# Two layers of a mixer and mixture-of-experts backbone on one core: an opening, a scan tail, a routing step and a gather put in another order

## The reference

```python
for l in range(DEPTH):
    sh1, sc1, g1, sh2, sc2, g2 = split(silu(c) @ w_ada[l] + b_ada[l], 6)     # modulation
    out = token_mixer(x * (1 + sc1) + sh1)         # attention, scan and gating branches
    x = layer_norm(alpha * x + g1 * out)
    ff = hier_moe(x * (1 + sc2) + sh2)             # 4 groups of 8 experts, two chosen
    x = layer_norm(alpha * x + g2 * ff)

def token_mixer(h):
    proj = h @ w_in                                # q, k, v, z, xbc, dt, u, gv, gates
    y_att, y_gm = attention(q, k, v), gelu(u) * spatial(layer_norm(gelu(gv)))
    y_ssm = rms_norm((scan(xbc, dt) + d * xs) * silu(z))
    return (g0 * (y_att @ wb[0]) + g1 * (y_ssm @ wb[1]) + g2 * (y_gm @ wb[2])) @ w_o
```

## Time and profile before

| | before |
|---|---|
| median of 3 runs (lowest, highest) | 1283.43 us (1276.03, 1285.51) |
| the profiled execution's own time | 1282.84 us |
| its span, first to last instruction | 1281.0 us |
| mean granted TensorE clock | 0.968 |
| PE busy | 1208.1 us (94%) |
| DVE busy | 971.0 us (76%) |
| ACT busy | 716.9 us (56%) |
| moved by DMA | 358.83 MB, mean 280 GB/s |

### The profile page before, as it was taken

How to read it: one execution, slowest core, us unless ns; L and a number is a source line. 1 busy time by engine, 2 the same in 40 slices (tenths; PEclk the granted TensorE clock), 3 DMA queues, 4 the chain that set the end, 5 groups by cost and what they waited for, 6 DMA issues and landing times.

```text
span 1281.0 us, 15755 instructions
## 1 busy us (share of the span) xinstructions
PE 1208.1 (94%) x5953; PEld 949.2 (74%) x5953; DVE 971.0 (76%) x1159; ACT 716.9 (56%) x684; POOL 74.5 (6%) x121
## 2 busy tenths in 40 slices
PE   4999999989989999999989999998998999999994
PEld 1667777877677888888767777776777888888883
DVE  1654657797689889888877475769857998888887
ACT  1543544553567777677753354445336776767773
POOL 0400000101000000000020000010000000000000
PEclk8899998999999999999989989989998999999998
DMA  9987763537899999999956767445348999999980
GB/s 355 291 287 274 296 229 139 184 137 273 333 356 363 375 369 353 347 370 346 343 166 227 293 242 282 163 139 175 136 169 306 369 397 354 357 338 371 347 321 34
DMA packets 99491, 358.83 MB, mean 280 GB/s; under 512 B 9188, under 2 KB 12736, under 8 KB 83024
## 3 DMA queue, kind: packets, MB, share of 16 engines
q1 hardware_dynamic: 87504, 295.12, 63.1%
q0 software_dynamic: 11904, 62.63, 13.9%
HBM read 352.92 MB, written 5.83 MB: 280 GB/s over the span
## 4 chain that ended last, share of the span: by engine, by line
PE 73%; DVE 11%; DMA 5%; ACT 4%; issue 2%; DVEq 2%; ACTq 1%; SPq 1%; POOL 0%; POOLq 0%
PE bank L950 69%; PE bank L953 4%; DVE wl L1826 4%; ACT wh L1521 2%; DMA adaw<-in_w_ada 2%; DMA first<-in_w_ada 1%; DMA raw<-in_w_in 1%; DVE tmp L1826 1%; DVE seg L2308 1%; DVEq L2333 1%; DMA decay<-decay_rows 1%; DVE xbc L2098 0%; DVE xbc L2095 0%; SPq L763 0%; DVE gv L1826 0%
## 5 line engine op out<-in xcount | busy, mean ns | idle before, releaser
L1826 DVE TENSOR_TENSOR wl<-raw,wh 128x2048 fp32r<-128x2048 f32 (+1 forms) x268 | 607.3, 2275 | 118.0 <-ACT wh L1521 64.6
L1731 ACT ACTIVATE wh<-raw 128x2048 fp32r<-128x2048 f32 x192 | 367.4, 1915 | 49.7 <-PE bank L950 34.9
L950 PE MATMUL bank<-wh,xgh 128*128 128x512 f32 x512 | 209.1, 408 | 0.6 <-ACT xgh L1766 0.6
L950 PE MATMUL bank<-wh,xgl 128*128 128x512 f32 x512 | 202.9, 396 | 0.0
L1521 ACT ACTIVATE wh<-raw 128x2048 fp32r<-128x2048 f32 (+1 forms) x76 | 142.2, 1872 | 103.8 <-PE bank L950 61.0
L950 PE MATMUL bank<-wh,hTh 128*128 128x512 f32 x448 | 184.5, 412 | 2.8 <-DVE wl L1826 2.0
L950 PE MATMUL bank<-wl,hTh 128*128 128x512 f32 x448 | 180.0, 402 | 0.0
L950 PE MATMUL bank<-wh,hTl 128*128 128x512 f32 x448 | 179.5, 401 | 0.0
L950 PE MATMUL bank<-wl,xgh 128*128 128x512 f32 x512 | 140.3, 395 | 0.0
L950 PEld LDWEIGHTS bank<-wl,xgh 128*128 128x128 f32 x512 | 96.0, 188 | 23.6 <-DVE wl L1826 0.4
L950 PEld LDWEIGHTS bank<-wh,xgh 128*128 128x128 f32 x512 | 96.8, 189 | 20.2 <-DVE xgl L1826 0.8
(11 more groups left out here) (301 smaller groups left out, 1465.6 us busy)
## 6 DMA issues: line engine op xcount, KB each, us to landing
raw<-in_moe_w SPq DMA_DIRECT2D x256, 512.0 KB, 5.6
raw<-in_moe_w SPq DMA_DIRECT2D x64, 1024.0 KB, 6.8
raw<-in_w_in SPq DMA_DIRECT2D x52, 1024.0 KB, 6.8
adaw<-in_w_ada POOLq DMA_DIRECT2D x32, 1024.0 KB, 6.7
raw<-in_w_branch SPq DMA_DIRECT2D x12, 1024.0 KB, 5.3
raw<-in_w_ada SPq DMA_DIRECT2D x8, 1024.0 KB, 9.9
raw<-in_w_o SPq DMA_DIRECT2D x8, 1024.0 KB, 4.9
first<-in_w_ada SPq DMA_DIRECT2D x4, 1024.0 KB, 16.7
```

What stands on the lines that cost most here:

```text
L950: return behind(nc.tensor.matmul(*args, **kw))
L1731: tally(A_(wh[c][:, :], slot[r], ACT.Copy), part_high[c])
L1826: return V.tensor_tensor(o, a, b, op)
```

## The change

Seven edits, in the order of the program:

1. SP fetches the last two `w_ada` chunks and the first q piece ahead of x, and x has semaphores of its own (`x_in`).
2. PE makes all eight chunks first; stream 0 of x is turned after them, stream 1 behind the first q products. ACT takes the modulation row ahead of the first q piece's high part, and makes the second piece's behind the first four rows of tokens; DVE does the modulation ahead of the first low part.
3. `scanned` no longer squares and sums on DVE; ACT does it (`squared`, an activation with an accumulator).
4. The low part of (2,1) moves on DVE from between the last two scan steps to behind `scanned(1)`.
5. PE makes half 1 of branch 2 for stream 0 ahead of turning z, and for stream 1 behind it.
6. The last two chunks of the next modulation move behind `rank` (layer 0); in layer 1 five mask products (`busy5`) stand there. ACT takes the row out behind the first two gathers of the loop.
7. The gate values' gather stands between the second and the third low product of expert 0's second half, not behind the products.

```diff
@@ sync, opening
-            sp.dma_start(x[:, 0, :], A["x_prompt"][0]).then_inc(once, 16)
-            sp.dma_start(x[:, 1, :], A["x_sample"][0]).then_inc(once, 16)
-            load(0, SLOTS)
             load_first(2)
             load_first(3)
+            load(0, SLOTS)
+            sp.dma_start(x[:, 0, :], A["x_prompt"][0]).then_inc(x_in[0], 16)
+            sp.dma_start(x[:, 1, :], A["x_sample"][0]).then_inc(x_in[1], 16)
@@ tensor
-            for key in ada(0, 0, 0, 6):
+            for key in ada(0, 0):
                 accumulate(0, "ada0", key)
-            pe.wait_ge(once, 48)
-            turn_x(0, "x1T")
-            for key in ada(0, 0, 6):
-                accumulate(0, "ada0", key)
+            pe.wait_ge(once, 16)
...
                 if l == 0:
+                    turn_x(l, "x1T", (0,))
                     turn_mod(l, 0, "adaT0")
                     keep_busy(l, "busy2", 6)
...
-                    if n == 1 and l:
+                    if n == 1:
                         turn_x(l, "x1T", (1,))
...
                 branch(l, 2, (0,))
+                branch(l, 2, (1,), (0,))
                 branch_rows(l, 1, z)
-                branch(l, 2, (1,))
+                branch(l, 2, (1,), (1,))
                 branch(l, 1)
...
                 turn_x(l, "x2T", (1,))
-                next_ada(6, 8)
                 pe.wait_ge(s0_act, 3 * l + 3)
...
                 fills(ins, "rank")
+                next_ada(6, 8)
+                if l == L - 1:
+                    keep_busy(l, "busy5", 5)
...
                             for c in range(4):
+                                if i == 0 and h == 1 and c == 2:
+                                    gather(tally, rnd, 0, SELECTED)
...
                             if rnd == 0 and l < L - 1:
                                 turn_mod(l, 0, "adaT_next")
-                            gather(tally, rnd, 0, SELECTED)
@@ scalar
-            convert_to(0, 0)
             take_row(0, 0, "ada0")
-            convert_to(0, 1)
+            convert_to(0, 0)
...
                         high(0, 2, 4)
+                        convert_to(l, 1)
...
+                def squared(s):
+                    act.wait_ge(z_scanned, 2 * l + s + 1)
+                    A_(tmp[:, NW:D], z[:, s, :], ACT.Square, accum_out=small[:, s:s + 1])
+                    act.drain().then_inc(z_squared, 1)
+                squared(0)
                 gate_take(1, 1)
                 branch_turned(2)
+                squared(1)
                 ahead(("branch", 2, 0))
                 square_root(1)
...
                 modulate("x2T", 1, lambda: root_of(0, 1))
-                if l < L - 1:
-                    take_row(l, 0, "ada_next")
...
                     gathered(0, 1)
+                    if rnd == 0 and l < L - 1:
+                        take_row(l, 0, "ada_next")
@@ vector
                 if l == 0:
+                    modulation(l, 0, "adaT0")
                     convert_to(0, 0)
-                    modulation(l, 0, "adaT0")
...
-                    tt(z[:, s, :], y, z[:, s, :], ALU.mult)
-                    drain()
-                    tt(tmp[:, NW:D], z[:, s, :], z[:, s, :], ALU.mult)
-                    drain()
-                    V.tensor_reduce(small[:, s:s + 1], tmp[:, NW:D], X, ALU.add)
-                    drain()
+                    tt(z[:, s, :], y, z[:, s, :], ALU.mult).then_inc(z_scanned, 1)
...
-                    if 1 <= n < 8:
+                    if 1 <= n < 7:
                         ahead(SCAN_FILL[n - 1])
...
                 scanned(1)
+                ahead(SCAN_FILL[6])
+                dve.wait_ge(z_squared, 2 * l + 2)
```

More of the change, by code:

```diff
@@ L240, in make_plan @@
         plan.append(("busy4", 4))
+        plan.append(("busy5", 4))
     plan.append(("rt", 5))
@@ L498, in hybrid_backbone @@
         once = sem("once")
+        x_in = [sem(f"x_in{s}") for s in range(2)]
         cond_in = sem("cond_in")
@@ L556, in hybrid_backbone @@
         y_sem = sem("y_sem")
+        z_scanned = sem("z_scanned")
+        z_squared = sem("z_squared")
         var_ready = sem("var_ready")
@@ L815, in _ @@
                 pool.wait_ge(first_in[i], 16)
+            for s in range(2):
+                pool.wait_ge(x_in[s], 16)
             for n in range(L):
@@ L1039, in turn_x @@
                 for s in streams:
-                    pe.wait_ge(x_norm[s], 2 * l + (which == "x2T") + 1)
+                    if l == 0 and which == "x1T":
+                        pe.wait_ge(x_in[s], 16)
+                    else:
+                        pe.wait_ge(x_norm[s], 2 * l + (which == "x2T") + 1)
                     xv = x[:, s, :].rearrange("t (p c) -> t c p", c=DC)
@@ L1094, in branch_rows, with branch @@
                     turn4(l, f"yT{b}{s}", [yv[:, c, :] for c in range(BC)])
-            def branch(l, b, halves_=(0, 1)):
+            def branch(l, b, halves_=(0, 1), streams=(0, 1)):
                 for n in halves_:
                     w = parts(l, ("branch", b, n), 512)
-                    for s in range(2):
+                    for s in streams:
                         if n == 0:
@@ L1106, in branch @@
                         fills(ins, f"br{b}{n}{s}")
-                    release(("branch", b, n))
+                    if 1 in streams:
+                        release(("branch", b, n))
             for s in part_free:
@@ L1522, in convert_to @@
                     cut[l] += 1
+            take_row(0, 0, "ada0")
             convert_to(0, 0)
-            take_row(0, 0, "ada0")
-            convert_to(0, 1)
             for l in range(L):
@@ L1834, in _ @@
             V.tensor_copy(cT[:, :, 0:2].rearrange("p c s -> p s c"), tmp[:, 0:16].rearrange("p (s c) -> p s c", s=2)).then_inc(c_ready, 1)
-            dve.wait_ge(once, 48)
+            dve.wait_ge(once, 16)
             for s in x_norm:
```

## The result

| | before | after |
|---|---|---|
| median of 12 runs (lowest, highest) | 1279.77 us (1274.88, 1285.51) | 1269.19 us (1263.87, 1273.79) |
| ratio, 95% interval | 1 | 0.9923 (0.9901 to 0.9946) |
| the profiled execution, its span | 1282.84, 1281.0 us | 1271.53, 1269.7 us |
| mean granted TensorE clock | 0.968 | 0.974 |

By the ratio the change takes off 9.9 us (6.9 to 12.7); the medians differ by 10.6. The sign was forecast; the size was not (5.1), and the time lies 1.8 under the range. Before itself came out lower than in the three runs ahead of the prediction: 1279.77 here, with those three among the 12, and 1277.7 to 1278.5 in the four later sets, against 1283.43.

The account below looks back on a forecast made before the run. PE was taken to hold 73% of the chain, so the change acts only where PE waits. Opening 0, scan tail -0.9 and -1.5, routing -2.4 and -0.3 sum to -5.1: 1282.84 to 1277.7 us, range 1271 to 1284.

Parts of the forecast that it names:

- scan tail: End of the scan, edits 3 to 5: -0.9 us in layer 0, -1.5 in layer 1, each between -2.8 and +1.4.
- Layer 0's routing: Edits 6 and 7: logits and first expert product 1.9 us earlier, gate values 0.5; -2.4, between -3.1 and -1.0.
- Layer 1's routing: Five mask products in the wait for `selg`, possibly ending up to 0.4 us late: -0.3, between -1.5 and +0.6.
- The opening: Edits 1 and 2: first q product near 38.1, gain lost in the attention's wait; 0, between -1.0 and +1.5 us.
- DVE's saving passes on whole: Rival, scan tail: 2.76 us gained per layer, 1274.6; decided by the scaled z starting 2 us or more earlier; 12%.
- The clock in layer 1's routing stays at the higher level: Rival, layer 1's routing: the 13.60 us stretch at clock 0.51 gets shorter, giving 1273.2; 10%.
- the change of layer 0's routing does nothing: Rival, layer 0: the following loop is bound by transfers, so the 2.4 us are not gained, 1280.1; 5%.
- The opening did not lose: Rival, opening: the slot freed 6 us later delays the loads of v, 3 us on top, 1280.7; 10%.
- The drain behind the table load: Rival, ACT's root in the scan tail: a drain of about 1.38 us delays the scaled z, 2.8 in both layers, 1280.5; 5%.
- The slower rival: Rival, scan tail: PE's new 1.8 us gap ahead of half 1 of branch 1 drops the clock, 6.8 us, 1284.5; 8%.

Follow-up runs that it names:

- weight_turn: The change with ACT's high part of branch 1 half 0 ahead of the second square and the branch order of before; ratio to before 0.9922.
- weight_first: The change with ACT's high part of branch 1 half 0 ahead of the second square; ratio to before 0.9901, a second time 0.9915.

## Why the prediction was wrong

**The base.** The sum was made on 1282.84 and a median of three runs, 1283.43. Five sets of 12 to 35 runs give 1277.7 to 1279.8. Of the 8.5 us by which 1277.7 lies above 1269.19, 3.1 are this (1282.84 - 1279.77), and an effect of 5.1 on 1279.77 would have been 1274.7. The measured 9.9 taken off 1282.84 would be 1272.9, inside the range.

**The clock was taken as unchanged.** This is the step that failed. Every wait of PE but the one in layer 1's routing went into the sum at its length; what the waits do to the clock stood among the rivals alone. In the four later sets of before (124 executions) the time is 8 to 9 us shorter for every 0.01 by which the mean granted clock of an execution is higher; the correlation is -0.89 to -0.94 in each set. The mean clock is 0.969 over these and 0.975 over the 22 executions of the change. At that price some 5 of the 9.9 us go with the clock, an estimate, and the 4 to 5 that remain are about what was forecast. This is a correlation: no run sets the clock by itself. Of the terms, the scan tail shows it most.

**The scan tail is the term that was mis-sized.** Forecast -0.9 and -1.5, together -2.4; timed alone -0.38% or 4.9 us (2.2 to 7.4). The traces agree: over six traces with the old tail and six with all three edits, the means are 76.6 and 74.2 in layer 0, 80.7 and 78.2 in layer 1, together -4.9. The steps themselves, the clock apart, were right: z 2.6 earlier (2.5 forecast), the scaled z 0.5 (0.2), the merges' waits gone, PE standing ahead of half 1 of branch 1 (1.11 us; 1.8 forecast). Two things were left out:
- *PE's waits were priced at their length alone.* All six old tails of layer 1 have a low stretch of the clock (the tail's mean is 0.96 to 0.98), and three of six in layer 0 (0.96); none of the six new ones has one in either layer. In layer 0 the old tails at the higher level are 75.7 to 76.0, those with a low stretch 77.0 to 77.7. So 1.6 of the 2.4 there is work and waiting, and 0.8 on the mean is the clock. In layer 1 four old tails take 80.5, and two with a low stretch twice as long 81.0; carried on to no low stretch this gives 80.0, so 1.8 of the 2.5 is work and waiting and 0.7 the clock, an estimate. Work and waiting are then 3.4, not the 2.4 of the sum, and the clock 1.5. I had weighed the clock only as a loss, through the new gap of PE; the waits for `W` that edits 3 and 4 take away (1.68 and 2.08 in the first trace of before, none in layer 0 of after) are of the same kind, and longer.
- *The parts were added as if each had a price.* Alone, edits 3 and 4 give nothing in the tails, and edit 5 makes them longer. The first two make a gap on PE, the third fills it.

That it is the waits which bring the clock down in these tails is a correlation over the 18 traces (weight_turn, whose wait ahead of the turn is 1.31 instead of 2.9 us, has no low stretch either). It was not isolated there, as the mask products do it for the gather of layer 1, by filling the waits with products that nobody uses.

**Layer 0's routing was right, at an undisturbed clock.** Forecast -2.4. At a clock of 1.00 the old routing takes 45.7 (three traces) and the new 43.4 (four): -2.3, of which the first expert product brings 1.7 and `hid` 0.6. On the mean of all traces with both edits or neither it is 46.4 to 44.4, -2.0, since low stretches fall into either. They fall in other places: without edit 6 the gather takes 5.4 us and more in five of eight traces; with it, the rank starts 2.9 to 3.4 us behind the start of the turning back in five of ten, and 1.9 in all others. One reading of the sum was wrong without harm: the two chunks are sixteen products and not eight, but products of 512 columns do start 0.23 apart, as from 347.91 on in the trace of after.

**Layer 1's routing: the size was right, the steps were not.** Forecast -0.3: a loss of 0.3, and 0.6 back if the clock rises within the gather. The five products cost nothing, since they end ahead of `selg` (0.79 us left of the wait), and the gather is at the higher level from its start (3.81 us, not 5.2 to 5.8). At the first expert product that is worth 0.4 to 0.7, and the means of the routing differ by 0.6.

**The opening was right**: the last chunk landed at 26.85 (forecast 27.2), the first q product started at 38.06 (38.1), and nothing is left at the attention; only the second q block came later, at 44.11 (43.1 to 43.5). In the openings of before and after SP's transfers landed in the order of their issue, as the sum takes it. It is no rule for the whole kernel: in the expert loops of before's trace 16 of them landed ahead of the one issued just before.

**Sum.** 0 - 4.9 - 2.0 - 0.6 = -7.5, inside the measured 6.9 to 12.7. The -0.6 is the difference of two means that scatter by 4. The 2.4 up to 9.9 are not placed; stretches that no edit touches differ by as much between two traces of one kernel (from layer 1's first q product to its tail, 214.3 and 212.0 us in the two of the change without the mask products), with their low stretches.

**The rivals.** "DVE's saving passes on whole" gave a time nearer the truth, for a wrong reason: its test, the scaled z 2 us earlier, was not met. "The clock in layer 1's routing stays at the higher level" came nearest, 1273.2. The trace of after looks like it, but the early low stretch that it lacks is not the edit's doing, and the gather alone is worth under 1 us; that the clock would count for half of the effect, all over the kernel, no rival had. That the change of layer 0's routing does nothing is refuted by its 2.0 to 2.3 and the loop behind it, which has the same length in all traces. The opening did not lose. The drain behind the table load did not show. Of "ScalarE: Activation LUTs", section "What ACT_TABLE_LOAD costs", in the Trainium skill, the trace of after agrees with the 1.28 us of the load and not with a drain on the road: the root starts 0.02 us behind it. The slower rival's gap came (1.11 us), but no low stretch followed it.

## What to carry to other kernels

When work is taken off one engine ahead of a hand-over, look at what the engine behind will do with the time, and move its filler in the same edit: here neither half gained in the tails, and both together gave 5 us. A few products in a wait directly ahead of a row of products can keep its clock up (a gather of 3.81 instead of 5.2 to 5.8 us here); look at what is left of that where the row's result is used (0.4 to 0.7). Before one stretch is compared between two traces, look at its granted clock in both; a difference of 4 us came and went with it in unchanged code. Take a second trace and a dozen times of the kernel before, before an effect of half a per cent is put on top of a base, and read the mean granted clock of each execution beside its time.

## What was not expected of the hardware

The low stretches of TensorE's clock move between executions of the same code, by as much as the change is worth. Over 35 executions of before the mean granted clock lies between 0.960 and 0.978 and the time between 1270.8 and 1288.8 us. The two traces of weight_first's kernel have layer 1's routing at 1.00 and 37.2 us, and at 0.92 and 40.4. In the 3.70 us at 953.3 above PE was busy the whole time at the lower level; in the 6.30 us ahead, at the higher one, it had been busy 4.37. Some places had one in every trace (layer 1's tail in all nine traces without the three edits together and without weight_turn's order on ACT), some in half of them.
